# A hybrid decoder step: the first output projection, the norm and the odd input projection as one stage

## The chip, the cores and the metric

One core of a Trainium2 chip runs the whole program. The metric is device time in microseconds (us), median of several executions; lower is better. TensorE is called PE, VectorE DVE, ScalarE ACT, GpSimd POOL, and SP is the engine that issues most DMA transfers. Every engine works through its own list of instructions in order and waits on semaphores.

## The reference, cut to what matters

Two layers are computed for 1024 prompt tokens and 64 sample tokens (T = 1088 rows, D = 1024 columns, all float32). The part between the layers is:

```
mix = concat(attention * silu(ga), hgrn * silu(gb))      # layer 0, T x 1024
y   = x + mix @ w_out_even[0]                            # 1024 x 1024
h   = y * rsqrt(mean(y*y, -1) + eps) * norm_g[1]         # RMS norm
q, k, v, g = split(h @ w_in_odd[0])                      # 1024 x 6144
```

Layer 0 begins in the same way, with h from the input x and w_in_even (1024 x 4096).

## The kernel before, in words

**Stages.** The program is a row of stages with a barrier behind each: project_in "even" (L93), attention, HGRN, project_out "out0" (L1638), project_in "odd" (L93 again), and retention with the last output projection. Rows are worked in NT = 9 tiles of 128 tokens (tile 8 has 64). The contraction of 1024 is cut in 8 chunks of 128.

**Precision.** A float32 operand a is split in hi = round(a) and lo = a - hi, both in the faster format fp32r, and a product is three matmuls: hi*hi, hi*lo, lo*hi. For the 64 rows of tile 8, hi and lo stand side by side as one stationary operand of 128 columns, so two matmuls do.

**project_out_alone (out0).** SP loads the weights in 8 chunks through 4 raw buffers (L1683) and the mix tiles through 2 (L1678). ACT rounds mix tiles (L1749) and even weight chunks (L1759), DVE subtracts (L1777, L1795), POOL does both for odd chunks (L1705, L1707). PE (L1720) makes tiles 0 and 1 together, chunk by chunk, as weights come; then one tile after another, 48 matmuls of 512 columns each. Tile 8 has 32. Two pairs of PSUM banks are used in turn. DVE adds the residual x (L1784, loaded by POOL's queue, L1698), ACT's queue stores y to DRAM (L1753).

**project_in.** SP loads ident and gain, then for odd cos and sin, then x tiles into 2 buffers (L195), with halves of the first weight blocks between (L197, L200). ACT squares and sums a tile (L386) and takes the root (L389). DVE inverts it (L495) and scales the 128x1024 tile to x_n (L499). PE transposes x_n in 8 pieces of 128x128 into two PSUM tiles, turn[0] and turn[1] (L236). DVE multiplies by the gain into h_f (L425), ACT rounds it to h_hi (L326), DVE subtracts to h_lo (L430). L433 places the lo of tile 8 beside its hi. POOL splits the weights by half blocks of 128x1024 (L223 rounds, L225 subtracts); a slot is two halves, and there are 4 slots.

**Units.** The products (L242) come in units of 24 matmuls (16 for the 64 rows) that each fill one of 6 PSUM banks. The first segment of odd is "rotary": unit u covers 362 or 364 tokens as moving columns; units 0 and 1 need the first 3 tiles, 2 and 3 the first 6, 4 and 5 all nine. Units 0 to 5 use slot 0, 6 to 11 slot 1. The first segment of even is "norm" with one unit of 512 columns per tile. "Early" units are made between the transposes, as soon as their tiles are there:

```python
            for t in range(NT):
                transpose_tile(t)
                while early < min(NBANK, early_units) and tiles_of(first, early) <= t - 1:
                    if early == 0:
                        pe.wait_ge(w_split, 4 if first in BY_TOKEN else 2)
                    pe.wait_ge(lo_done, 2 * tiles_of(first, early))
                    unit(first, first_at, 0, 0, early)
                    early += 1
            pe.wait_ge(lo_done, 2 * NT + 2)
```

The rest follows in order, PE waiting for a bank to be emptied (`free`) and for w_split. Rotary units are emptied by DVE (L481 to L489).

**The order of the work** around the change is written out by hand: each engine's list is fixed, and the semaphores (m_split, full, added, turned, hi_done, lo_done, w_split) only hold it back.

Of the kernel before, what the change touches and what calls it, by code (L numbers as in the profile page):

```python
# [13 lines left out]

# [12 lines left out]
P = 128  # L27
# [62 lines left out]
NSTAGE = 3  # L90


def project_in(nc, tag, x_of, gain_dram, weight, segments, consts, qk_gain_dram=None):  # L93
# [6 lines left out]
    with nc.cleanup_on_exit(), ExitStack() as ctx:  # L100
        sb = lambda n, s, d=F32: ctx.enter_context(nc.sbuf_tensor(f"{tag}_{n}", s, d))
        sem = lambda n: nc.alloc_semaphore(f"{tag}_{n}")
        even = tag == "even"
        bank = [ctx.enter_context(nc.psum_tensor(f"{tag}_bank{i}", [P, 512], F32)) for i in range(NBANK)]
# [5 lines left out]
        x_in = sb("x_in", [P, 2, D])  # L110
        x_n = sb("x_n", [P, 2, D])
        square = sb("square", [P, D])
# [4 lines left out]
        h_f = sb("h_f", [P, 2, 4, P])  # L117
# [5 lines left out]
        stage_tm = sb("stage_tm", [P, NSTAGE, 2 * WBLK])  # L123
        if even:
            stage_fm = sb("stage_fm", [P, 2, T])
            qk_gain = sb("qk_gain", [P, 2, DA])
# [5 lines left out]
        else:  # L132
# [3 lines left out]
            rot = sb("rot", [P, 4, 364])  # L136

        const_in = sem("const_in")
        x_load = [sem("x_load0"), sem("x_load1")]
        sumsq_done, std_done, rstd_done, xn_done = sem("sumsq"), sem("std"), sem("rstd"), sem("xn")  # L140
        turned, gained, hi_done, lo_done = sem("turned"), sem("gained"), sem("hi"), sem("lo")
# [13 lines left out]
        NCONST = 16 * 4  # L155
# [15 lines left out]

        @contextmanager
        def two_by_two(engine, n):

            assert n == 1 or n % 2 == 0
            if n <= 2:
                yield [(i, i) for i in range(n)]
            else:
                with engine.Fori(0, n // 2) as i:
                    yield [(2 * i + sub, sub) for sub in range(2)]  # L180

        @block.sync
        def _(sp):
            sp.dma_start(ident[:], consts["ident"]).then_inc(const_in, 16)
            sp.dma_start(gain[:], gain_dram, allow_slow_non_contiguous=True).then_inc(const_in, 16)
            if even:
                for i in range(2):
                    sp.dma_start(qk_gain[:, i, :], qk_gain_dram[i].to_broadcast([P, DA])).then_inc(const_in, 16)
            else:
                sp.dma_start(cos[:], consts["cos"]).then_inc(const_in, 16)  # L190
                sp.dma_start(sin[:], consts["sin"]).then_inc(const_in, 16)
            for t in range(NT):
                if t >= 2:
                    sp.wait_ge(xn_done, t - 1)
                sp.dma_start(x_in[0:rows_of(t), t % 2, :], x_of(t)).then_inc(x_load[t % 2], 16)  # L195
                if t in (1, 2):
                    sp.dma_start(raw[:, t - 1, :, :], w_rows[:, 4 * (t - 1):4 * t, 0:WBLK]).then_inc(raw_in[t - 1], 16)  # L197
                if t in (3, 4):
                    sp.wait_ge(w_split, t - 2)
                    sp.dma_start(raw[:, t - 3, :, :], w_rows[:, 4 * (t - 3):4 * (t - 2), WBLK:2 * WBLK]).then_inc(raw_in[t - 3], 16)  # L200
# [8 lines left out]
        def _(pool):  # L209

            pool.sem_inc(w_used, 2)
            with pool.Fori(0, NBLK // NSLOT) as turn_of_slots:
                for slot in range(NSLOT):
# [3 lines left out]
                    for half in range(2):  # L217
                        r = raw[:, half, :, :]
                        hi = w_hi[:, slot, half * 4:half * 4 + 4, :]
                        lo = w_lo[:, slot, half * 4:half * 4 + 4, :]  # L220
                        pool.wait_ge(raw_in[half], 16 * NSLOT * turn_of_slots + 16 * slot + 16)
                        pool.sem_inc(w_at_hand, 1)
                        nc.gpsimd.tensor_copy(hi, r).then_inc(w_hi_done, 1)  # L223
                        pool.wait_ge(w_hi_done, 2 * NSLOT * turn_of_slots + 2 * slot + half + 1)
# [2325 lines left out]
```

## Time and profile before

| | us |
|---|---|
| median of 3 runs | 2255.38 (2255.22 to 2260.37) |
| the profiled execution | 2255.49 |
| its span in the profile | 2253.8 |
| PE busy | 1957.6 (87%) |
| DVE busy | 966.5 (43%) |
| POOL busy | 654.8 (29%) |
| ACT busy | 528.9 (23%) |

In the profile, an instruction has a start and a duration. A float32r matmul of 512 columns lasts 0.39 us at the full clock, but the next one starts 0.23 after it, since matmuls are pipelined; what counts is the distance of the starts. PEclk is the clock granted to PE (1.00 is 2.4 GHz, 0.50 is 1.2 GHz). "idle before <-X" is how long the engine stood still and what released it. The program has 28678 instructions.

### The profile page before, as it was taken

To read this page: it belongs to the slowest core of one execution; us is meant where nothing else is said; L and a number is where in the kernel's file an instruction comes from. 1 tells how busy PE (TensorE), PEld (TensorE's weight loads), DVE (VectorE), ACT (ScalarE), POOL (GpSimd) and SP (SyncE) were. 2 spreads that over 40 slices of the span, in tenths; PEclk is the share of its full clock that TensorE was granted. 3 is DMA by queue.
4 is the path that set the end of the run, shared out by engine and by line. 5 is a ranking of instruction groups with operands and counts; after the bars stand their busy time and mean duration, and the time that the engine had idled before them with its cause. 6 is when DMAs were issued, how large, how long until landed. Compare 5 with 4: busy or idle time off the path is not lost. (4 is left out here: it accounts for less than half of the span.)

```text
span 2253.8 us, 28678 instructions
## 1 busy us (share of the span) xinstructions
PE 1957.6 (87%) x10146; PEld 1570.9 (70%) x10146; DVE 966.5 (43%) x1465; ACT 528.9 (23%) x1018; POOL 654.8 (29%) x556
## 2 busy tenths in 40 slices
PE   5999999788787864876884999999999949999998
PEld 4788998744444534764774999888788836777776
DVE  5650001087874448893327544211100035656564
ACT  3210110166554343332103000000011122323231
POOL 2522222065553006550204322233222032212120
PEclk9999999888888986796996999999999969999999
DMA  4332221233420653112425223223322187655553
GB/s 131 109 109 79 88 87 59 81 104 121 121 93 26 192 173 98 50 52 94 161 98 175 87 87 98 90 85 108 96 82 68 49 239 217 204 182 187 185 175 117
DMA packets 209185, 262.33 MB, mean 116 GB/s; under 512 B 22901, under 2 KB 149557, under 8 KB 208821
## 3 DMA queue, kind: packets, MB, share of 16 engines
q1 hardware_dynamic: 153396, 202.15, 29.1%
q10 hardware_dynamic: 53680, 53.50, 7.3%
q0 software_dynamic: 2000, 5.25, 0.8%
q8 instruction: 67, 1.10, 0.2%
q14 instruction: 42, 0.34, 0.1%
HBM read 179.31 MB, written 79.17 MB: 115 GB/s over the span
## 5 line engine op out<-in xcount | busy, mean ns | idle before, releaser
L242 PE MATMUL odd_bank<-odd_w_hi,odd_h_hi 128*128 128x512 f32 x576 | 224.9, 390 | 2.5 <-DVE odd_stage_tm L470 2.5
L242 PE MATMUL odd_bank<-odd_w_lo,odd_h_hi 128*128 128x512 f32 x576 | 224.6, 390 | 0.0
L242 PE MATMUL odd_bank<-odd_w_hi,odd_h_lo 128*128 128x512 f32 x512 | 199.9, 390 | 0.0
L223 POOL CAST odd_w_hi<-odd_raw 128x1024 fp32r<-128x1024 f32 x48 | 53.8, 1120 | 386.7 <-PE odd_bank L242 322.7
L242 PE MATMUL even_bank<-even_h_hi,even_w_hi 128*128 128x362 f32 (+1 forms) x384 | 126.9, 330 | 4.5 <-DVE even_stage_tm L470 4.5
L242 PE MATMUL odd_bank<-odd_h_hi,odd_w_hi 128*128 128x362 f32 (+1 forms) x384 | 127.4, 332 | 2.2 <-DVE odd_h_hi L433 2.2
L242 PE MATMUL odd_bank<-odd_h_lo,odd_w_hi 128*128 128x362 f32 (+1 forms) x384 | 127.0, 331 | 0.0
L242 PE MATMUL even_bank<-even_h_hi,even_w_lo 128*128 128x362 f32 (+1 forms) x384 | 126.7, 330 | 0.0
L242 PE MATMUL even_bank<-even_h_lo,even_w_hi 128*128 128x362 f32 (+1 forms) x384 | 126.6, 330 | 0.0
L242 PEld LDWEIGHTS odd_bank<-odd_w_hi,odd_h_hi 128*128 128x128 f32 x576 | 108.5, 188 | 25.4 <-DVE odd_stage_tm L470 3.0
L242 PE MATMUL odd_bank<-odd_h_hi,odd_w_lo 128*128 128x362 f32 (+1 forms) x384 | 126.2, 329 | 0.0
L242 PE MATMUL even_bank<-even_w_hi,even_h_hi 128*128 128x512 f32 x288 | 114.7, 398 | 12.4 <-POOL even_w_lo L225 7.6
L242 PEld LDWEIGHTS odd_bank<-odd_w_lo,odd_h_hi 128*128 128x128 f32 x576 | 108.6, 188 | 22.5
L225 POOL TENSOR_TENSOR odd_w_lo<-odd_raw,odd_w_hi 128x1024 fp32r<-128x1024 f32 x48 | 117.1, 2440 | 3.8
L1539 PE MATMUL hg_sc<-hg_x 128*128 128x128 f32 x448 | 72.7, 330 | 50.7 <-DVE hg_x L1439 33.9
L242 PE MATMUL even_bank<-even_w_lo,even_h_hi 128*128 128x512 f32 x288 | 113.5, 394 | 0.0
L242 PEld LDWEIGHTS odd_bank<-odd_w_hi,odd_h_lo 128*128 128x128 f32 x512 | 96.4, 188 | 20.2
L1539 PEld LDWEIGHTS hg_sc<-hg_x 128*128 128x128 f32 x448 | 68.2, 241 | 57.9 <-issue 52.1
L647 POOL CAST ap_k_hi<-ap_sums 128x512 fp32r<-128x512 f32 (+3 forms) x96 | 48.3, 503 | 198.9 <-DVEq L788 134.6
L223 POOL CAST even_w_hi<-even_raw 128x1024 fp32r<-128x1024 f32 x32 | 36.0, 1125 | 235.1 <-PE even_bank L242 188.3
L2148 PE MATMUL rt_y<-rt_w_hi,rt_m_hi 128*128 128x512 f32 x256 | 103.3, 404 | 0.0
L242 PE MATMUL even_bank<-even_w_hi,even_h_lo 128*128 128x512 f32 x256 | 101.1, 395 | 0.0
(302 smaller groups left out, 4419.9 us busy)
## 6 DMA issues: line engine op xcount, KB each, us to landing
odd_raw<-in_w_in_odd SPq DMA_DIRECT2D x48, 512.0 KB, 3.9
even_raw<-in_w_in_even SPq DMA_DIRECT2D x32, 512.0 KB, 3.8
k_page<-in_cache_k SPq DMA_DIRECT2D x64, 256.0 KB, 3.1
v_page<-in_cache_v SPq DMA_DIRECT2D x64, 256.0 KB, 3.0
rt_s<-in_state_ret SPq DMA_DIRECT2D x32, 512.0 KB, 6.0
out_ret_sample<-rt_s SPq DMA_DIRECT2D x32, 512.0 KB, 3.2
v_tm<-odd_stage_tm ACTq DMA_DIRECT2D x64, 128.0 KB, 1.9
g_tm<-odd_stage_tm ACTq DMA_DIRECT2D x64, 128.0 KB, 1.9
```

The lines of the kernel that those rows point to most:

```text
L223: nc.gpsimd.tensor_copy(hi, r).then_inc(w_hi_done, 1)
L225: nc.gpsimd.tensor_tensor(lo, r, hi.bitcast(F32), ALU.subtract).then_inc(w_split, 1)
L242: mm = pe.matmul(out, stationary, moving, start=(j == 0), stop=(j == len(pairs) - 1))
L647: nc.gpsimd.tensor_copy(k_hi[:, m, lo:NQ], sums[:, i % NX, lo:NQ]).then_inc(carry_hi, 1)
L1539: mm = pe.matmul(sc[2 * (l % 2) + c // 4][:, c % 4, :], lhs[:, tok], rhs[:, tok], start=True, stop=True)
L2148: mm = pe.matmul(yp[half][:], a[:, r, :], b[:, r, cols], start=(r == 0 and j == 0), stop=(r == R - 1 and j == len(ops) - 1))
```

## The change

It does four things.

1. project_out_alone is gone. project_in "odd" does its work first, in the same stage: the buffers of the later part (w_hi, w_lo, stage_rot, stage_tm, rot) serve as weight and mix buffers of the output projection. y stays in x_in (and is stored to DRAM too, for the last stage).
2. The three pairs of the six banks are used for the products. Tiles 2 to 6 are made one by one; transposes of an earlier tile stand among their products. Tiles 7 and 8 are made together, chunk by chunk (row by row of the weights), so that POOL can overwrite used weight chunks with the first odd weights.
3. In both input projections the tile isn't scaled before the transpose. PE multiplies the unscaled tile by diag(rstd) (128x128), a float32 matmul, which transposes and scales at once. x_n goes.
4. h_f goes as well: ACT (with the gain as scale) and DVE read the PSUM tile in 4 pieces each per half. project_in "even" has 4 input buffers instead of 2.

The diff, cut to its core:

```diff
-        x_n = sb("x_n", [P, 2, D])
-        h_f = sb("h_f", [P, 2, 4, P])
+        nx = NX if even else 2          # NX = 4
+        diag = sb("diag", [P, 2, P])
+        def o_bank(t, n):
+            return bank[2 * (t % 3) + n]
@@ block.sync
             if even:
...
+                for t in range(NT):
+                    if t >= nx:
+                        sp.wait_ge(turned, 2 * (t - nx + 1))
+                    sp.dma_start(x_in[0:rows_of(t), t % nx, :], x_of(t)).then_inc(x_load[t % nx], 16)
+                    if t in (1, 2):
+                        load_raw(0, t - 1)
+                    if t in (3, 4):
+                        sp.wait_ge(w_split, t - 2)
+                        load_raw(1, t - 3)
             else:
+                def load_mix(t):
+                    if t >= 2:
+                        sp.wait_ge(m_split, t - 1)
+                    sp.dma_start(mix[:, t % 2, :, 0:r], ...).then_inc(mix_in[t % 2], 16)
+                for c in range(KD):
+                    if c >= NRAW:
+                        sp.wait_ge(*split_by(c - NRAW))
+                    sp.dma_start(oraw[:, c % NRAW, :], ow_rows[:, c, :]).then_inc(oraw_in[c % NRAW], 16)
+                    if c < 2:
+                        load_mix(c)
+                    if c == 2:
+                        load_consts()
+                for t in range(2, NT):
+                    load_mix(t)
+                    if t in (3, 4):
+                        load_raw(0, t - 3)
+                sp.dma_start(cos[:], ...); sp.dma_start(sin[:], ...)
+                for half in range(2):
+                    sp.wait_ge(w_split, half + 1)
+                    load_raw(1, half)
@@ block.gpsimd
+            def load_residual(t):
+                if t >= 2:
+                    pool.wait_ge(y_left[t % 2], 16 * (t // 2))
+                    pool.wait_ge(turned, 2 * (t - 2) + 2)
+                pool.dma_start(x_in[0:rows_of(t), t % 2, :], out.x_of(t)).then_inc(res_in[t % 2], 16)
+            if not even:
...
+                for t in range(2, NT):
+                    load_residual(t)
+                for slot in range(NSLOT):
+                    if slot < NSLOT - 1:
+                        pool.wait_ge(chunk_used, 2 * slot + 2)
+                    else:
+                        pool.wait_ge(o_full, NT)
+                    split_slot(0, slot)
@@ block.tensor
-                        mm = pe.transpose(turn[k][:, c, 0:r], x_n[...], ident[0:r, 0:r])
+                        mm = pe.matmul(turn[k][:, c, 0:r], x_in[0:r, t % nx, (4 * k + c) * P:(4 * k + c + 1) * P],
+                                       diag[0:r, t % 2, 0:r], start=(c == 0), stop=True, skip_group_check=True)
+            def first_chunk(t):
+                pe.wait_ge(m_split, t + 1)
+                if t >= 3:
+                    pe.wait_ge(added, t - 2)
+            def project_tiles():
+                for c in range(KD):
+                    for t in range(2):
+                        if c == 0:
+                            first_chunk(t)
+                        if t == 0:
+                            pe.wait_ge(*split_by(c))
+                        mm = chunk(t, c)
+                        if c == KD - 1:
+                            mm.then_inc(o_full, 1)
+                for t in range(2, NT - 2):
+                    first_chunk(t)
+                    for c in range(KD):
+                        mm = chunk(t, c)
+                        if c == KD - 3:
+                            transpose_tile(0 if t == 2 else t - 1)
+                    mm.then_inc(o_full, 1)
+                    if t == 2:
+                        transpose_tile(1)
+                first_chunk(NT - 2)
+                first_chunk(NT - 1)
+                for c in range(KD):
+                    mm = chunk(NT - 2, c)
+                    if c == KD - 1:
+                        mm.then_inc(o_full, 1)
+                    mm = chunk(NT - 1, c)
+                    mm.then_inc(o_full if c == KD - 1 else chunk_used, 1)
+                    if c == 4:
+                        transpose_tile(NT - 3)
+            else:
+                project_tiles()
+                early_unit(0)
+                transpose_tile(NT - 2)
+                early_unit(1)
+                transpose_tile(NT - 1)
+                for early in range(2, 4):
+                    early_unit(early)
@@ block.scalar
-                nc.scalar.copy(h_hi[:, 4 * k:4 * k + 4, ...], h_f[:, k, :, 0:r]).then_inc(hi_done, 1)
+                for c in range(4 * k, 4 * k + 4):
+                    ins = nc.scalar.activation(h_hi[:, c, ...], turn[k][:, c % 4, 0:r], ACT.Copy, scale=gain[:, c:c + 1])
+                ins.then_inc(hi_done, 1)
+            def split_hi(t):
+                act.wait_ge(mix_in[t % 2], 16 * (t // 2) + 16)
+                if t >= 2:
+                    act.wait_ge(o_full, t - 1)
+                nc.scalar.copy(m_hi[...], mix[...]).then_inc(m_hi_done, 1)
+                split_hi(0)
+                round_weights(0)
+                split_hi(1)
+                for c in range(2, KD, 2):
+                    round_weights(c)
+                act.wait_ge(const_in, NCONST)
+                split_hi(2)
+                split_hi(3)
+                for t in range(2):
+                    norm(t)
+                    store(t)
+                cast(0)
+                for t in range(4, NT):
+                    cast(t - 3)
+                    split_hi(t)
+                    norm(t - 2)
+                    store(t - 2)
+                cast(NT - 3)
+                for t in range(NT - 2, NT):
+                    norm(t)
+                    store(t)
+                cast(NT - 2)
+                cast(NT - 1)
@@ block.vector
-                dve.tensor_scalar(x_n[0:r, t % 2, :], x_in[0:r, t % 2, :], rstd[0:r, t:t + 1], None, ALU.mult)
+                dve.tensor_scalar(diag[0:r, t % 2, :], ident[0:r, :], rstd[0:r, t:t + 1], None, ALU.mult).then_inc(diag_done, 1)
+                    for c in range(4 * k, 4 * k + 4):
+                        ins = dve.scalar_tensor_tensor(h_lo[:, c, ...], turn[k][:, c % 4, 0:r], gain[:, c:c + 1],
+                                                       h_hi[:, c, ...], ALU.mult, ALU.subtract)
+                for t in range(4, NT):
+                    gain_and_split(t - 3)
+                    add(t - 2)
+                    scale(t - 2)
+                    split_lo(t)
```

## Rows read from the trace of the kernel before

**Rows 1.** The page, first part: busy time and share of each engine.

```profile
PE 1957.6 (87%) x10146; PEld 1570.9 (70%) x10146; DVE 966.5 (43%) x1465; ACT 528.9 (23%) x1018; POOL 654.8 (29%) x556
```

**Rows 2.** Stretches around the seam: us, busy of each engine, PEclk, DMA share, GB/s.

```profile
1098.50:1175.40 76.90, 74.59 (x328) 61.11 (x326) 17.75 (x24) 6.93 (x7) 3.73 (x7) 1.00 0.39 130
1175.40:1194.30 18.90, 0.00 (x0) 0.00 (x0) 4.30 (x8) 4.06 (x7) 1.60 (x2) 0.63 0.49 160
1194.30:1215.90 21.60, 9.33 (x40) 7.87 (x41) 20.42 (x23) 9.37 (x18) 14.07 (x7) 0.50 0.58 189
...
1247.00:1421.00 174.00, 174.00 (x1055) 174.00 (x1056) 77.45 (x138) 0.00 (x0) 42.42 (x24) 1.00 0.28 82
```

**Rows 3.** Timeline of PE, end of the seam: start, us, instruction, idle before and its releaser.

```profile
1246.95 0.43 PE L242 MATMUL odd_bank<-odd_h_hi,odd_w_hi 128*128 128x362 f32 x1 [2.17 <-DVE odd_h_hi L433]
```

**Rows 4.** Timeline of ACT, DVE and PE at the start of out0.

```profile
1066.23 1.04 ACT L1749 CAST out_m_hi<-out_mix 128x1024 fp32r<-128x1024 f32 x1 [9.85 <-DMA out_mix<-mix]
...
1070.60 1.04 ACT L1749 CAST out_m_hi<-out_mix 128x1024 fp32r<-128x1024 f32 x1 [3.33 <-DMA out_mix<-mix]
...
1073.34 5.35 DVE L1795 TENSOR_TENSOR out_w_lo<-out_raw,out_w_hi 128x1024 fp32r<-128x1024 f32 x2
...
1075.54 1.19 PE L1720 MATMUL out_bank<-out_w_hi,out_m_hi 128*128 128x512 f32 x2 [19.80 <-DVE out_w_lo L1795]
```

**Rows 5.** Timeline of out0: PE at tile 2; DVE's split of tile 8 and addition of tile 6.

```profile
1102.50 0.73 PE L1720 MATMUL out_bank<-out_w_hi,out_m_hi 128*128 128x512 f32 x2 [2.25 <-DVE out_xy L1784]
...
1157.95 0.69 DVE L1777 TENSOR_TENSOR out_m_hi<-out_mix,out_m_hi 128x512 fp32r<-128x512 f32 x1 [8.03 <-ACT out_m_hi L1749]
1158.56 1.28 DVE L1784 TENSOR_TENSOR out_xy<-out_bank,out_xy 128x512 f32<-128x512 f32 x2
```

**Rows 6.** Timeline of PE in the even stage: transposes between two units.

```profile
40.01 1.03 PE L236 MATMUL even_turn<-even_ident,even_x_n 128*128 128x128 f32 x8
40.80 0.47 PE L242 MATMUL even_bank<-even_w_hi,even_h_hi 128*128 128x512 f32 x1
```

**Rows 7.** Timeline of PE: 16 records of full float32 matmuls, two per matmul.

```profile
1017.50 1.95 PE L1539 MATMUL hg_sc<-hg_x 128*128 128x128 f32 x16
...
1034.50 3.64 PE L1572 MATMUL hg_o<-hg_v,hg_kd_tm 128*128 128x128 f32 x16
```

**Rows 8.** Timeline of ACT and DVE: the norm of tiles in the odd stage.

```profile
1198.83 1.05 ACT L386 ACTIVATE odd_square<-odd_x_in 128x1024 f32<-128x1024 f32 x1
...
1200.54 0.76 DVE L499 TENSOR_SCALAR odd_x_n<-odd_x_in,odd_rstd 128x1024 f32<-128x1024 f32 x1
...
1229.10 2.64 DVE L499 TENSOR_SCALAR odd_x_n<-odd_x_in,odd_rstd 128x1024 f32<-128x1024 f32 x1
```

**Rows 9.** Groups by line and shape: 128x128 operations out of PSUM, mean ns last.

```profile
L2264 ACT CAST rt_ms<-rt_tr 128x128 fp32r<-128x128 f32 x8 | 2.1, 266 | 29.4 <-PE rt_tr L2109 29.4
...
L1490 DVE SCALAR_TENSOR_TENSOR hg_state<-hg_state,hg_eb,hg_o 128x128 f32<-128x128 f32 x28 | 9.7, 348 | 1.3 <-PE hg_o L1572 0.2
```

**Rows 10.** Timeline of out0: first store of y, and the residual load behind it.

```profile
1102.64 0.34 ACTq L1753 DMA_DIRECT2D y<-out_xy  x1
...
1108.59 0.57 POOL L1698 DMA_DIRECT2D out_xy<-in_x_prompt  x1 [18.83 <-DMA y<-out_xy]
```

**Rows 11.** Timeline of PE: the even stage's pause before unit 6.

```profile
76.67 0.76 PE L242 MATMUL even_bank<-even_w_hi,even_h_hi 128*128 128x512 f32 x1 [4.15 <-DVE even_head_n L461]
...
81.08 0.43 PE L242 MATMUL even_bank<-even_w_lo,even_h_hi 128*128 128x512 f32 x1
```

**Rows 12.** Timeline of POOL in the even stage: weight halves, and PE's first product.

```profile
11.06 1.04 POOL L223 CAST even_w_hi<-even_raw 128x1024 fp32r<-128x1024 f32 x1 [10.49 <-DMA even_raw<-in_w_in_even]
12.18 2.35 POOL L225 TENSOR_TENSOR even_w_lo<-even_raw,even_w_hi 128x1024 fp32r<-128x1024 f32 x1
20.51 1.04 POOL L223 CAST even_w_hi<-even_raw 128x1024 fp32r<-128x1024 f32 x1 [5.98 <-DMA even_raw<-in_w_in_even]
...
32.42 0.79 PE L242 MATMUL even_bank<-even_w_hi,even_h_hi 128*128 128x512 f32 x1 [7.64 <-POOL even_w_lo L225]
```

More of the change, by code:

```diff
@@ L13 @@
 from contextlib import ExitStack, contextmanager
+from dataclasses import dataclass
 import numpy as np
@@ L90 @@
 NSTAGE = 3
+NX = 4
+_held = {}
+@dataclass
+class OutFirst:
+    mix_fm: object
+    weight: object
+    x_of: object
+    y_of: object
 def project_in(nc, tag, x_of, gain_dram, weight, segments, consts, qk_gain_dram=None):
@@ L216, in _ @@
                         pool.wait_ge(w_used, 2 * turn_of_slots + slot // 2 + 2)
[L217 to L224, printed above, removed]
-                        nc.gpsimd.tensor_tensor(lo, r, hi.bitcast(F32), ALU.subtract).then_inc(w_split, 1)
+                    split_slot(turn_of_slots, slot)
         @block.tensor
@@ L288, in _, with chunk @@
             early_units = UNITS[first] if first in BY_TOKEN else UNITS[first] // 2
-            for t in range(NT):
-                transpose_tile(t)
-                while early < min(NBANK, early_units) and tiles_of(first, early) <= t - 1:
-                    if early == 0:
-                        pe.wait_ge(w_split, 4 if first in BY_TOKEN else 2)
-                    pe.wait_ge(lo_done, 2 * tiles_of(first, early))
-                    unit(first, first_at, 0, 0, early)
-                    early += 1
+            def chunk(t, c):
+                hi, lo = m_hi[:, t % 2, c, :], m_lo[:, t % 2, c, :]
+                ops = ((hi, ow_hi), (hi, ow_lo), (lo, ow_hi)) if t < NT - 1 else ((hi, ow_hi), (hi, ow_lo))
+                for j, (m, w) in enumerate(ops):
+                    for n in range(2):
+                        mm = pe.matmul(o_bank(t, n)[:], m, w[:, c, n * 512:n * 512 + 512],
+                                       start=(c == 0 and j == 0), stop=(c == KD - 1 and j == len(ops) - 1))
+                return mm
@@ new lines, in early_unit @@
+            def early_unit(u):
+                if u == 0:
+                    pe.wait_ge(w_split, 4 if first in BY_TOKEN else 2)
+                pe.wait_ge(lo_done, 2 * tiles_of(first, u))
+                if not even:
+                    pe.wait_ge(added, NT - 2 + u // 2)
+                unit(first, first_at, 0, 0, u)
+            if even:
+                for t in range(NT):
+                    transpose_tile(t)
+                    while early < min(NBANK, early_units) and tiles_of(first, early) <= t - 1:
+                        early_unit(early)
+                        early += 1
+            else:
[5 more added lines that the diff above has]
+                for early in range(2, 4):
+                    early_unit(early)
+                early = 4
@@ L380, in act_unit, with norm @@
                     act.dma_start(sample[head], stage_rot[:, s, :, TP:T]).then_inc(left_fm[s], 16)
-            act.wait_ge(eps_set, 1)
-            for t in range(NT):
+            def norm(t):
                 r = rows_of(t)
-                act.wait_ge(x_load[t % 2], 16 * (t // 2 + 1))
-                nc.scalar.activation(square[0:r, :], x_in[0:r, t % 2, :], ACT.Square,
+                if even:
+                    act.wait_ge(x_load[t % nx], 16 * (t // nx + 1))
+                else:
+                    act.wait_ge(added, t + 1)
+                nc.scalar.activation(square[0:r, :], x_in[0:r, t % nx, :], ACT.Square,
                                      accum_out=ssum[0:r, t:t + 1]).then_inc(sumsq_done, 1)
@@ L408, in _ @@
                 act.wait_ge(left_fm[i], (16 if even else 48) * (fm // 2) + 16)
+            if not even:
+                act.wait_ge(y_left[0], 16 * (NT // 2 + 1))
+                act.wait_ge(y_left[1], 16 * (NT // 2))
         @block.vector
@@ L1808 @@
-_held = {}
 def retention(nc, *args):
```

346 lines of the change are left out of this document (146 added, 200 removed).

## The prediction

> **What bounds the kernel now.** I read the share of each engine first [rows 1]: TensorE (PE) is busy 87% of the span, the next engine 43%. So the kernel is a chain of stages that PE bounds, and a change pays where PE stands still or is slow. Next the stretches around the seam [rows 2]. The first output projection runs from 1075.5 to 1175.4, nearly without a pause. Then PE does nothing for 18.9 us and runs at the lower clock level (granted 0.50, which is 1.2 GHz) for 21.6 more; from 1247 on it is busy 174.0 of 174.0 us. The last part of the seam ends at 1246.95 [rows 3], 71.6 us after the products. In it lie the transposes of nine tiles in pieces, each behind VectorE (the last wait is 2.17 for L433), and, by the order of the code, four units (0 to 3) of the odd input projection. A unit of 24 matmuls takes 24 x 0.165 = 4.0 us (1055 records in 174.0 us [rows 2]), four take 15.9. The other 55.7 us are what the seam costs: the y tiles go to DRAM, a barrier, the reload, the norm. The output products stand 0.227 us apart (328 in 74.6 [rows 2]); a tile of 48 takes 10.9, a chunk of six 1.36.
>
> **Start of the merged stage.** Today PE starts at 1075.5 behind the second mix tile and then the first weight split [rows 4]: ScalarE rounds mix 0 at 1066.2 and mix 1 at 1070.6, when its transfer lands, and only then the weights. The new order is mix 0, weight chunk 0, mix 1. Chunk 0 was issued before mix 0, so I take it as landed by 1067.3: rounding to 1068.3, VectorE's subtraction until about 1071.0 (5.35 for two in its row, beside GpSimd), PE from 1071.1, 4.4 us earlier. The second tile's split, ready about 1073.4, meets PE's first six products (6 x 0.43 at the lower level). Bounds 0 (weights land late) and 5; I take 4.4.
>
> **The hand-over to tile 2.** Today a gap of 2.25 [rows 5]: PE waits for rounding, split and the addition that frees the banks. With three bank pairs the addition goes; what stays is rounding 1.04 [rows 4] plus a split of 1.2 (twice the 0.69 of half the size [rows 5], less overlap) after tile 0's last product, less the 1.36 of tile 1's last chunk: about 1.0. Gain 1.2.
>
> **The transposes become products with diag(rstd).** Eight transposes of a tile take 0.79 of PE (40.01 to 40.80 [rows 6]). The new form is a full fp32 matmul, two records for each of 128 columns. 16 such records in a row take 1.95 including the last one's drain, so about 1.75 of PE time at the upper level; at the lower one 3.64 and 3.4 [rows 7]. Seven tiles (0 to 6) now stand among the projection's products: 7 x 1.75 = 12.3 us added there. A rule speaks against this. The Trainium skill, page "TensorE: Matmul & The Clock Gate", section Terms, has transposes in transpose mode four times as fast for FP32; by it a tile's products would take 4 x 0.79 = 3.2, not 1.75. The rows of this kernel say a factor near two, and I go by them.
>
> **Is each norm done in time?** For tile t the chain after its last product is addition 1.3 [rows 5], then square to the start of the scaling 1.7 [rows 8], then diag, an operation of 128x128 and some 0.3 (0.35 for the nearest of that size [rows 9]). In all 3.3, where PE has six chunks of the next tile, 8.2 us. Gain and split of a tile are now 8 ScalarE and 8 VectorE instructions of 128x128 out of PSUM, 0.27 and 0.35 each [rows 9], overlapping to about 1.0 per half; they lie behind the next products. The residual load waits for the store two tiles back (issue 1102.64, POOL goes on 1108.59, 6 us [rows 10]) and has over 12. The first pair is the tightest. Its products end at 1099.9 - 4.4 = 1095.5, tile 2 runs from 1096.5, so transposes 0 are due at 1096.5 + 8.2 = 1104.7 and transposes 1 at 1104.7 + 1.75 + 2.7 = 1109.1. Addition 0 follows split 2 (1096.5 to 1097.8), and with the norm and a table load diag 0 is there at 1101; the halves of tile 0 are rounded from 1106.3 and split by 1108.6 and 1110, each when its bank is due. All at nothing, with 2 to 8 us of cover; without cover each us late is a us of PE.
>
> **The stall that the change adds.** Tiles 7 and 8 start together, and tile 8's mix shares its buffer with tile 6. So ScalarE may round it only when tile 6 is complete, and VectorE has addition 6 and scaling 6 (which waits for ScalarE's norm 6) queued ahead of split 8: 1.35 + 1.8 + 0.3 + 0.7 [rows 5, 8, 9] + the start of PE 0.15 = 4.3 us in which PE has nothing; transposes 6 and units wait behind it. The same length of pause in the even stage (4.15) left PE at the lower level: ten products at 0.43 instead of 0.23 [rows 11], 2.0 us. Together 6.3. Bounds: 3 (a quicker queue, no clock loss) and 9.
>
> **The end of the stage.** Products end at 1175.4 - 4.4 - 1.2 + 12.3 + 6.3 = 1188.4. Unit 0, transposes 7, unit 1, transposes 8, units 2 and 3 follow: 15.9 + 1.75 + 1.3 (64 rows) = 19.0. Diag 7 is due 4.0 after the end and ready at 2.5; its VectorE operation has only SBUF operands, and such ones take up to 2.64 instead of 0.76 beside GpSimd [rows 8], so up to 1 more, which the wait of unit 0 below covers. With the 1.0 that unit 0 waits (next part) unit 4 starts at 1208.4 instead of 1246.95. **Gain 38.5 us.** After that the stage is PE alone, as before.
>
> **The queues.** SP issues ident and gain behind weight chunk 2 (used by ScalarE at mix 2, some 15 us later), the two halves of the first odd block behind mix 3 and 4, cos and sin behind mix 8, which goes out when tile 6's mix is split, about 1152; VectorE wants them at 1203. Then SP waits for the splits from 1174 on, with only the next weight halves behind it. POOL has the residual loads ahead of the new splits; the last of them (tile 8) waits for transposes 6, some 5 us before the end of the products, and that is later than the use of chunk 1. So the new splits start only near 1182, at 3.5 us (1.04 and 2.35 [rows 12]) to 4 each, and two of them end near 1189.4: unit 0, due at 1188.4, waits 1.0 us for them (bounds 0 and 3). Unit 6 gets its four near 1197 and needs them at 1216. The old barrier, the reload and the nine x loads of SP go.
>
> **The even stage** changes too. Four input buffers let x 2 and the second weight half be asked for at once. Today that half reaches GpSimd at 20.5 after 6 us of waiting, and the fourth split ends at 32.4, which starts PE [rows 12]. With the transfers back to back (x 0, x 1 and the first half, 1.5 MB, were in by 11.06) the second half lands by 14.6, and the four splits end near 14.6 + 3.8 + 3.9 + 3.9 = 26.2. Transposes 2 end near 25, so PE starts at 26.3: 6.1 earlier. Against this stand 5 x 0.95 + 0.6 = 5.4 for transposes 3 to 8, which lie between units, and 0.5 for the smaller instructions in the pause before unit 6 [rows 11]. Sum -0.2; bounds -5 and +5.
>
> **Sum.** The profiled execution took 2255.5 (span 2253.8 and 1.7 around it), the median of the three runs is 2255.4. 2255.5 - 38.5 - 0.2 = 2216.8.
>
> **Rivals.**
> 1. The hand-overs are dearer: weights land late at the start (4.4 lost), a missed norm or two in the first pair, diag 7 and 8 behind GpSimd. Each is 1 to 5 us; for it speaks the tight first pair, against it the cover elsewhere. 7 to 19 us less gain: 2224 to 2236, middle 2229. Chance 0.17.
> 2. The products with diag take four times today's 0.79, so 3.2 a tile: 1.45 more for 9 tiles in the merged stage and 6 in the even one, some 20 us: 2237. This is the mechanism behind the rule cited above. Against it stand 16 records in 1.95. Chance 0.03.
> 3. Slower: the chain through VectorE's queue (gain and split, addition, the wait for the norm, split of the next mix tile) takes longer than PE's 12.7 us a tile (10.9 + 1.75). Then PE pauses at every tile boundary as at tile 8, 4.3 plus 2.0 of clock. For tiles 2 to 8 that is 44 us against 38.5 gained: 2261. It decides from 12.7 + 4.3 = 17 us of chain on; my sum from complete tile to split is 4.3, with the gain and split 6.5. Chance 0.03.
> 4. The seam does not close: the transposes are issued in order on PE, so a norm late for its slot in every tile would keep the 12.3 and give back half of the 55.7. 2240 or so. Chance 0.02.
> 5. More gain: the stall at tile 8 short, the clock kept, the even start 5 better: 2206. Chance 0.07, and 0.68 for the forecast's own 2209 to 2224.
>
> The range 2206 to 2236 holds case 1 and the forecast with its unknown bounds (5 at the start, 3 at the stall, 5 in the even stage). A measurement of this kernel tells about 0.3%, 7 us, from no change. Faster by more than that: all but 3, and a little of unseen trouble, 0.95; within 0.02; slower 0.03.
>
> **What would show it.** PE's first product of the merged stage near 1071; 16 records of diag products in 1.95; a pause near 1 us before tile 2; no pause over 0.5 us at tiles 3 to 7; one pause near 4.3 before tile 7 with slow products behind it; continuous PE from there, a wait of 1 us at unit 0, unit 4 near 1208; in the even stage the first product at 26 and the pause before unit 6 near 4.6. The forecast is wrong if PE waits for diag or split in each tile, or if 16 records take over 3 us.

## The result, and the profile after

The changed kernel takes **2218.74 us** (median of 4, 2217.01 to 2219.43) against 2255.3 (2254.49 to 2260.37) for the kernel before on the same chip: ratio 0.983 [0.9815, 0.9849]. Predicted were 2216.8 in a range of 2206 to 2236. A later series gave 2220.5 (2219.6 to 2233.6, 6 runs) against 2257.99, ratio 0.984 [0.9809, 0.987]. The profiled execution took 2217.01 (span 2215.2). In the profile TensorE (PE) is busy for slightly longer, and still not for the whole span:

```profile
PE 1959.9 (88%) x10290; PEld 1577.1 (71%) x10290; DVE 931.5 (42%) x1537; ACT 547.0 (25%) x1126; POOL 646.4 (29%) x556
```

PE's busy time grew by 2.3 us [rows 1]; the span fell by 38.6. So time in which PE stood still went away, and the windows of the changed kernel say where (columns as in [rows 2]):

```profile
1057.60:1069.80 12.20, 0.04 (x1) 0.04 (x1) 3.46 (x4) 3.88 (x4) 4.39 (x4) 0.50 0.98 309
1069.80:1094.00 24.20, 24.06 (x96) 19.30 (x96) 6.34 (x5) 3.40 (x5) 13.05 (x7) 0.92 0.52 173
1094.00:1161.20 67.20, 66.07 (x336) 55.75 (x336) 29.84 (x79) 28.10 (x73) 3.21 (x6) 1.00 0.45 151
1161.20:1165.30 4.10, 0.00 (x0) 0.02 (x1) 2.28 (x5) 2.05 (x4) 0.00 (x0) 1.00 0.34 140
1165.30:1186.40 21.10, 21.09 (x93) 17.48 (x94) 2.17 (x9) 2.18 (x8) 5.29 (x5) 0.92 0.08 23
1186.40:1208.00 21.60, 20.38 (x130) 19.59 (x129) 13.86 (x34) 6.89 (x22) 17.86 (x11) 1.00 0.54 166
```

From 1069.8 to 1208.0 PE is busy 131.6 of 138.2 us; between products and odd projection it had done nothing for 18.9 and been busy for only 9.33 of the next 21.6, at granted 0.50 [rows 2]. The rows of PE that answer to [rows 3 to 7, 11], from its timeline:

```profile
27.64 0.50 PE L342 MATMUL even_bank<-even_w_hi,even_h_hi 128*128 128x512 f32 x1 [1.79 <-POOL even_w_lo L292]
...
75.92 0.77 PE L342 MATMUL even_bank<-even_w_hi,even_h_hi 128*128 128x512 f32 x1 [4.42 <-DVE even_head_n L670]
...
1069.77 1.22 PE L394 MATMUL odd_bank<-odd_w_hi,odd_m_hi 128*128 128x512 f32 x2 [17.23 <-DMA odd_gain<-in_norm_g]
...
1095.04 0.74 PE L394 MATMUL odd_bank<-odd_w_hi,odd_m_hi 128*128 128x512 f32 x2 [1.17 <-DVE odd_m_lo L714]
...
1118.01 1.95 PE L336 MATMUL odd_turn<-odd_diag,odd_x_in 128*128 128x128 f32 x16
1119.71 0.71 PE L394 MATMUL odd_bank<-odd_w_hi,odd_m_hi 128*128 128x512 f32 x2
1120.27 0.62 PE L394 MATMUL odd_bank<-odd_w_lo,odd_m_hi 128*128 128x512 f32 x2
...
1130.34 0.62 PE L394 MATMUL odd_bank<-odd_w_hi,odd_m_lo 128*128 128x512 f32 x2
1130.80 1.95 PE L336 MATMUL odd_turn<-odd_diag,odd_x_in 128*128 128x128 f32 x16
...
1165.31 0.71 PE L394 MATMUL odd_bank<-odd_w_hi,odd_m_hi 128*128 128x512 f32 x2 [4.21 <-DVE odd_m_hi L714]
1165.86 0.99 PE L394 MATMUL odd_bank<-odd_w_lo,odd_m_hi 128*128 128x512 f32 x2
1166.65 1.05 PE L394 MATMUL odd_bank<-odd_w_hi,odd_m_lo 128*128 128x512 f32 x2
...
1188.49 0.43 PE L342 MATMUL odd_bank<-odd_h_hi,odd_w_hi 128*128 128x364 f32 x1 [1.22 <-POOL odd_w_lo L292]
...
1200.40 0.43 PE L342 MATMUL odd_bank<-odd_h_hi,odd_w_hi 128*128 128x362 f32 x1
...
1208.40 0.33 PE L342 MATMUL odd_bank<-odd_h_hi,odd_w_hi 128*128 128x362 f32 x1
```

Unit 2 starts at 1200.40 and, 48 products later, unit 4 at 1208.40: 38.6 earlier than [rows 3]. That equals the gain of the whole span, so nothing behind the seam gives or takes. But part of it is chance. The stage's first DMA went out at 1057.60; in the trace of before it was at 1060.82:

```profile
1057.60 0.34 SPq L259 DMA_DIRECT2D odd_stage_rot<-in_w_out_even  x1
...
1062.46 0.48 SPq L231 DMA_DIRECT2D odd_gain<-in_norm_g  x1
```

Counted from it, unit 4 came after 186.13 us before and after 150.80 now: the merged stage gives **35.3**. In the profiles of the changed kernel and the twelve runs below this first DMA lay between 1057.60 and 1078.34, though attention and HGRN, which stand ahead of it, are the same in all. That is why effects of a few us are read below from **local stretches** of one execution. I use D (the stage's first DMA), T2 (first product of tile 2) and U2 (first product of unit 2, behind transposes 8). For the changed kernel U2 - D = 142.80 and U2 - T2 = 105.36; its second profile gave 144.36 and 106.06. Up to T2, eight of the profiles have the same merged stage: T2 - D lies between 37.03 and 38.88 in them (37.44 in the changed kernel's). From T2 to U2, five have the same waits and code: 105.36 to 106.51. One execution can't tell an effect smaller than these spreads of 1.9 and 1.2 by its length alone; a wait that is there or gone can still be read from its row.

### The profile page after: what moved, and what is told of

Same layout as the page of the kernel before. It is cut to its first block and busy times, and to the rows that moved or that the text cites. A ratio compares the mean times of both kernels' runs of the same rounds, so it can differ in the third digit from the quotient of the medians.

```text
span 2215.2 us, 29001 instructions
## 1 busy us (share of the span) xinstructions
PE 1959.9 (88%) x10290; PEld 1577.1 (71%) x10290; DVE 931.5 (42%) x1537; ACT 547.0 (25%) x1126; POOL 646.4 (29%) x556
```

## The experiments

**Which part of the change pays?** Two kernels each keep one half. e1_even_only has the new even stage and the old project_out_alone and odd stage; e2_even_old is the reverse:

```diff
 # e1_even_only
-project_in(nc, "odd", ...)            # merged
+project_out_alone(nc, "out0", ...)    # as before
+project_in_old(nc, "odd", ...)
 # e2_even_old
-project_in(nc, "even", ...)
+project_in_old(nc, "even", ...)
```

> The even stage as changed, the output projection and the odd stage as before. My account of the gain puts it all at the seam: the even stage gives at most 1 us, so 2254 to 2256, no difference that can be measured, and the stretch from the first weight transfer of the output projection to unit 4 of odd stays 186.1 us. Rival: the 2.5 us by which HGRN ended earlier in the changed kernel are owed to the even stage; then 2251 to 2253.

> The merged stage as changed, the even stage as before. The seam account: 2218 to 2221, with unit 4 of odd 150.7 us after the first weight transfer of the output projection as in the changed kernel, and unit 6 of even at 76.7 instead of 75.9. Rival (the even stage has a share): 2222 to 2224.

Measured: e1 2261.65 (2255.64 to 2265.19) against 2256.23, ratio 1.001 [0.9992, 1.0027]. Its median lies above the 2254 to 2256 that I expected, but the ratio shows no change, and unit 4 of odd came 186.40 after D (186.1 expected). Unit 6 of even came at 76.23, before 76.67 [rows 11]; e2, with the old even stage, has it at 76.19. e2 2219.31 (2218.06 to 2221.66), ratio 0.9829 [0.9794, 0.9865]; U2 - D 143.54, PE's pauses behind its start within 0.1 of the changed kernel's. All of the gain that can be measured is the merged stage; the new even stage pays for itself and no more.

**The start.** The prediction had PE start when weight chunk 0 is split. The timeline of VectorE (DVE) says that this split was done at 1066.3, and PE started 3.5 later:

```profile
1065.05 1.22 DVE L718 TENSOR_TENSOR odd_w_lo<-odd_stage_rot,odd_w_hi 128x1024 fp32r<-128x1024 f32 x1
...
1161.14 1.29 DVE L726 TENSOR_TENSOR odd_x_in<-odd_bank,odd_x_in 128x512 f32<-128x512 f32 x2 [0.32 <-PE odd_bank L394]
...
1163.97 0.16 DVE L703 RECIPROCAL odd_rstd<-odd_std 128x1 f32<-128x1 f32 x1 [1.54 <-ACT odd_std L552]
1164.17 0.29 DVE L707 TENSOR_SCALAR odd_diag<-odd_ident,odd_rstd 128x128 f32<-128x128 f32 x1
1164.37 0.68 DVE L714 TENSOR_TENSOR odd_m_hi<-odd_shared,odd_m_hi 128x512 fp32r<-128x512 f32 x1
```

The row of PE at 1069.77 names gain: PE waits at its head for all constants, and SP issued gain as the seventh transfer of the stage, at 1062.46, behind three weight chunks, two mix tiles and ident, while the DMA engines were full (share 0.98 in the first window). e3_no_const_wait takes that wait out of PE's head in the odd stage; ScalarE still has it, ahead of anything that makes diag:

```diff
-            pe.wait_ge(const_in, NCONST)
+            if even:
+                pe.wait_ge(const_in, NCONST)
```

> PE's wait for ident and gain stands only in the even stage; in the merged one PE starts with the products (its transposes wait for diag anyway). If that wait alone held the first product, PE starts when chunk 0 is split, 3 us earlier (some 8.8 instead of 12.2 after the first transfer), then pauses 1 to 2 us for tile 1's split, so that unit 4 comes 1.5 to 2 us earlier; the whole 2215 to 2218. Rival: the weight chunks become the bound at once, and unit 4 doesn't move.

Measured (one execution, 2235.63, whose extra time lies ahead of the stage: D at 1078.34):

```profile
1088.07 1.19 PE L395 MATMUL odd_bank<-odd_w_hi,odd_m_hi 128*128 128x512 f32 x2 [14.79 <-DVE odd_w_lo L719]
...
1092.41 0.73 PE L395 MATMUL odd_bank<-odd_w_hi,odd_m_hi 128*128 128x512 f32 x2 [1.45 <-DVE odd_m_lo L715]
```

PE starts 9.73 after D instead of 12.17, and 0.15 after VectorE has split chunk 0 (3.5 before), so the wait was what held it. But it then runs into the second mix tile, which was due next (1.45). A wait removed uncovers the next one: of the 2.4 at the start, 1.3 are left at tile 2 (T2 - D 36.12 for 37.44; the least of the eight profiles with the wait is 37.03). At U2 0.2 is left (142.63 for 142.80), since in this execution the slow products behind the later stall went on longer (granted 0.74 over 1184.7 to 1196.0), and the edit doesn't touch those. So what it is worth alone at the end of the stage isn't shown; at tile 2 it is 0.9 to 2.8 against those eight.

**The stall before tiles 7 and 8.** The four last rows of VectorE above are the predicted chain: addition 6, the wait for norm 6, the scaling, and only then split 8; PE has nothing for 4.21. Two kernels attack it. e4_apart makes tile 8 after tile 7 instead of together with it, so PE has 48 products to do meanwhile; e5_split_first moves split 8 ahead in VectorE's queue:

```diff
 # e4_apart
-                for t in range(2, NT - 2):
+                for t in range(2, NT - 1):
...
-                first_chunk(NT - 2)
                 first_chunk(NT - 1)
                 for c in range(KD):
-                    mm = chunk(NT - 2, c)
...
-                    if c == 4:
-                        transpose_tile(NT - 3)
 # e5_split_first, in VectorE's list
                     gain_and_split(t - 3)
+                    if t == NT - 1:
+                        split_lo(t)
                     add(t - 2)
                     scale(t - 2)
-                    split_lo(t)
+                    if t < NT - 1:
+                        split_lo(t)
```

> Tiles 7 and 8 are made one after the other, as tiles 2 to 6. My account of the stall: mix 8 is split beside tile 7, so the 4.2 us pause and the slow products behind it (1.9) go, 6.1 us; GpSimd still gets chunk 1 free some 5.5 us before the end of the products, so unit 0 waits 1 to 2 us as now. Unit 4 comes 5 to 6 us earlier, the whole 2211 to 2214. Rival, the reason for making them together: the weights are freed too late, unit 0 waits over 5 us, and nothing is won: 2217 to 2220.

> VectorE splits mix 8 ahead of addition 6 and scaling 6 instead of behind them; nothing else changes. If its queue makes the 4.2 us pause, the pause is what rounding and split alone take, 0.62 + 0.68 and some 0.2: about 1.5 us, and the products behind it stay at 0.23 (pauses of 1.2 left the clock up). From the first product of tile 2 to unit 4 some 4.5 us less. Rival: the pause comes from ScalarE or from the mix transfer and stays 4.2.

e4: 2217.28 (2214.47 to 2217.59), ratio 0.9813 [0.9778, 0.9849]. Its windows and PE's row at unit 0:

```profile
1099.18:1185.30 86.12, 86.12 (x432) 72.59 (x432) 34.99 (x94) 32.76 (x86) 8.85 (x11) 1.00 0.41 136
```
```profile
1187.09 0.43 PE L342 MATMUL odd_bank<-odd_h_hi,odd_w_hi 128*128 128x364 f32 x1 [1.76 <-POOL odd_w_lo L292]
```

PE is busy 86.12 of 86.12 us at granted 1.00; U2 - T2 is 99.82, 5.5 less, and unit 0 waits 0.5 more for weights, since the chunks come free later. So the stall with its slow products costs 6.1, as the prediction had it (6.3). The total is not the 2211 to 2214 that I expected, but the stage also began late in this profile (D at 1062.15, 4.55 later). e5 (one execution, 2221.39, D at 1063.85):

```profile
1170.17 0.70 PE L394 MATMUL odd_bank<-odd_w_hi,odd_m_hi 128*128 128x512 f32 x2 [1.69 <-DVE odd_m_hi L714]
```
```profile
1170.17:1180.00 9.83, 9.83 (x43) 8.09 (x44) 1.40 (x4) 1.45 (x3) 0.00 (x0) 1.00 0.13 53
```

This is a pause of 1.69 (1.5 expected) with granted 1.00 behind it, where 4.21 was followed by products some 0.42 apart until 1169.2; U2 - T2 = 101.22, 4.1 less (4.5 expected), of which 2.5 is the shorter pause and 1.6 the clock. Both kernels fit the account of the prediction: the price is the pause and, nearly half as much again, the slow products that follow it.

**Unit 0's weights.** GpSimd's timeline in the changed kernel:

```profile
24.11 1.04 POOL L290 CAST even_w_hi<-even_raw 128x1024 fp32r<-128x1024 f32 x1 [2.10 <-DMA even_raw<-in_w_in_even]
...
1180.94 0.53 POOL L298 DMA_DIRECT2D odd_x_in<-in_x_sample  x1 [21.52 <-PE odd_turn L336]
1181.46 1.05 POOL L290 CAST odd_w_hi<-odd_raw 128x1024 fp32r<-128x1024 f32 x1
...
1186.06 2.37 POOL L292 TENSOR_TENSOR odd_w_lo<-odd_raw,odd_w_hi 128x1024 fp32r<-128x1024 f32 x1
```

GpSimd stood 21.52 behind the residual load of tile 8, which waits for transposes 6, though chunks 0 and 1 were free before. e8_residual_sp lets SP issue that one load:

```diff
 # SP, behind cos and sin
+                sp.wait_ge(y_left[0], 16 * ((NT - 1) // 2))
+                sp.wait_ge(turned, 2 * (NT - 3) + 2)
+                sp.dma_start(x_in[0:TS, 0, :], out.x_of(NT - 1)).then_inc(res_last, 16)
 # GpSimd
-                for t in range(2, NT):
+                for t in range(2, NT - 1):
                     load_residual(t)
```

> The residual of tile 8 is asked for by SP instead of GpSimd's queue, so that GpSimd can split the first odd weights as soon as chunk 1 of the last pair is used. If the wait for transposes 6 in GpSimd's queue sets the 1.2 us wait of unit 0, the splits start near 13 us after the pause's end less 7 (at 6 instead of 16 us), unit 0 doesn't wait, unit 4 comes 1.2 earlier. Rival: the weights aren't there or the new pause moves to transposes 7 (diag 7), same unit 4.

GpSimd's first split now starts 7.3 us after the end of the stall instead of 16.2, and the wait of 1.2 at unit 0 is gone, in one execution (2220.98); U2 - T2 is 104.82, only 0.5 less, as the slow products behind the stall lasted 0.7 longer this time.

**The even stage.** The fourth weight half was asked for only at 19.01, because SP first waited to load x 4 into a freed buffer. e7_even_order puts both halves ahead of x 4:

```diff
-                    if t in (3, 4):
-                        sp.wait_ge(w_split, t - 2)
-                        load_raw(1, t - 3)
+                    if t == 3:
+                        for half in range(2):
+                            sp.wait_ge(w_split, half + 1)
+                            load_raw(1, half)
```

> Even stage: SP asks for the second half of weight block 1 before x tile 4, whose wait for transposes 0 held it in the queue until 18.6. The half is asked for at 18.1, the fourth split ends 0.9 us earlier, PE's first product of even comes at 26.7 to 27.2 instead of 27.6, bound then by transposes 2. Unit 6 0.5 to 0.9 earlier. Rival: PE's start is bound by transposes 2 already, no change.

Unit 6 starts at 74.05 instead of 75.92 (total 2222.27 in one execution):

```profile
22.23 1.04 POOL L291 CAST even_w_hi<-even_raw 128x1024 fp32r<-128x1024 f32 x1 [0.24 <-DMA even_raw<-in_w_in_even]
...
25.77 0.50 PE L343 MATMUL even_bank<-even_w_hi,even_h_hi 128*128 128x512 f32 x1
...
74.05 0.77 PE L343 MATMUL even_bank<-even_w_hi,even_h_hi 128*128 128x512 f32 x1 [4.43 <-DVE even_head_n L671]
```

That is 1.9 less, where I expected 0.5 to 0.9. The fourth split begins at 22.23 instead of 24.11, and PE's first product comes at 25.77 instead of 27.64. SP asked for the half only about 1 us earlier; the other 0.9 was won between the issue and the split, and why isn't shown (x 4 no longer goes ahead of it).

**Diag products against transposes.** e9_transpose keeps the merged stage but scales rows to x_n and transposes them in transpose mode, with x_n in a buffer that is free then:

```diff
-                        mm = pe.matmul(turn[k][:, c, 0:r], x_in[...], diag[0:r, t % 2, 0:r], start=(c == 0), stop=True, ...)
+                        mm = pe.transpose(turn[k][:, c, 0:r], x_n[0:r, t % 2, ...], ident[0:r, 0:r])
...
-                dve.tensor_scalar(diag[0:r, t % 2, :], ident[0:r, :], rstd[0:r, t:t + 1], None, ALU.mult)
+                dve.tensor_scalar(x_n[0:r, t % 2, :], x_in[0:r, t % 2, :], rstd[0:r, t:t + 1], None, ALU.mult)
```

> The merged stage scales the tile on VectorE and transposes it on PE in transpose mode, as the kernel before did, instead of the product with diag; the even stage keeps diag. A tile's transposes take 0.8 of PE instead of 1.9: 7 x 1.1 among the products, 1.1 and 1.4 for tiles 7 and 8, against it 0.5 more in the pause before tile 7. Unit 4 comes 9 to 10 us earlier, the whole 2208 to 2211. Rival: VectorE's dearer scaling (0.76, up to 2.6 beside GpSimd) makes PE wait for the tiles 0, 1, 7 and 8, and half of it is lost: 2212 to 2216.

Measured: 2220.87 (2216.49 to 2227.24), ratio 0.984 [0.9817, 0.9864], where 2208 to 2211 was expected: no faster than the changed kernel in total. PE's rows:

```profile
1128.15 1.04 PE L341 MATMUL odd_turn<-odd_ident,odd_stage_rot 128*128 128x128 f32 x8
...
1140.03 1.03 PE L341 MATMUL odd_turn<-odd_ident,odd_stage_rot 128*128 128x128 f32 x8
...
1172.26 1.19 PE L399 MATMUL odd_bank<-odd_w_hi,odd_m_hi 128*128 128x512 f32 x2 [4.73 <-DVE odd_m_hi L722]
...
1205.58 0.43 PE L341 MATMUL odd_turn<-odd_ident,odd_stage_rot 64*128 64x64 f32 x4 [0.59 <-DVE odd_h_lo L641]
```

A tile step is 11.88 (1128.15 to 1140.03) instead of 12.79, 0.91 less. In both kernels the 48 products of a step stand 0.229 apart and take 10.99 (in the changed kernel 44 of them in the 10.07 from 1120.27 to 1130.34), so the transposes take 0.89 and the diag form 1.80. But the scaling of 1024 columns lies in the chain of the stall (4.73 instead of 4.21), the products behind it were slow for longer (1.3 in this execution), and 0.59 + 0.60 of waits appear at tile 8. U2 - T2 = 100.04, 5.3 less where 9 to 10 was expected.

**Put together.** c3_lead takes e3, e5, e7 and e8, and lets the first tile of each pair run ahead of the second (by one chunk at tiles 0 and 1, by two at 7 and 8), so that PE has products while the second mix tile is split. c4_lead_transpose adds e9. a1_after is the changed kernel again, beside them on the same chip:

```diff
+            def ahead(t0, t1, lead):
+                order = [(t0, c) for c in range(lead)]
                 for c in range(KD):
-                    for t in range(2):
+                    order += [(t0, c + lead)] * (c + lead < KD) + [(t1, c)]
+                return order
...
+                for t, c in ahead(0, 1, 1):
...
+                for t, c in ahead(NT - 2, NT - 1, 2):
```

> The changed kernel once more, as the measure for the two beside it: 2217 to 2220, unit 2 of odd begins 142.8 us after the first weight transfer of the output projection.

> All that the single runs showed, together: no constants wait for PE, mix 8 split first, residual 8 by SP, the even weight half before x 4, and in both pairs of tiles the first runs ahead (one chunk in the first pair, two in the last), so that the second's split lies beside products. If each pause is what the single runs made of it: first product 9.7 instead of 12.2 after the first transfer, no pause at tiles 1, 2, 7, 8 and unit 0; 2.4 + 1.2 + 6.1 + 1.2 less, unit 2 at 131.9 instead of 142.8; 1.9 in the even stage; in all 12.8 less than the changed kernel: 2206. Rival: the early start runs into the weight chunks, which come as before, and 2 to 4 us of it come back: 2208 to 2210.

> The same with transposes of the scaled tile in the merged stage instead of products with diag. Each takes 0.97 of PE instead of 1.91 (tile steps of 11.85 and 12.79), nine of them 8.5 less if none waits: unit 2 at 124, the whole 2198. Rival: transposes 8 wait for VectorE (1.2 as in the single run) and those of tiles 0 and 1 too; 4 us come back, 2202.

| | us | ratio to before | U2 - D |
|---|---|---|---|
| a1_after | 2220.5 | 0.984 [0.9809, 0.987] | 144.36 |
| c3_lead | 2210.47 | 0.979 [0.9758, 0.9822] | 132.12 |
| c4_lead_transpose | 2206.37 | 0.9767 [0.9738, 0.9795] | 126.85 |
| c5_mixed | 2201.52 | 0.9744 [0.9722, 0.9766] | 124.92 |

The stretch of c3 came out as expected (132.12 for 131.9), its total didn't (2210.47 for 2206; the rival had 2208 to 2210). c4 missed both (126.85 for 124, 2206.37 for 2198): its rival, waits at transposes 8, is part of it. c5, tried after these two, stands in the last row.

The windows of c3 show the waits at the second mix tile and before tiles 7 and 8 filled:

```profile
1068.10:1094.00 25.90, 25.54 (x98) 20.06 (x99) 10.46 (x7) 5.40 (x6) 16.45 (x9) 0.89 0.64 203
1094.00:1180.00 86.00, 86.00 (x435) 72.83 (x434) 34.22 (x93) 33.54 (x87) 11.57 (x12) 1.00 0.43 142
1180.00:1207.40 27.40, 27.40 (x177) 27.10 (x176) 16.05 (x38) 5.44 (x19) 19.30 (x11) 1.00 0.45 144
```

In c4, PE waited before transposes 8, and VectorE's timeline says for what:

```profile
1183.26 0.43 PE L346 MATMUL odd_turn<-odd_ident,odd_stage_rot 64*128 64x64 f32 x4 [2.88 <-DVE odd_h_lo L652]
...
1184.30 0.43 PE L346 MATMUL odd_turn<-odd_ident,odd_stage_rot 64*128 64x64 f32 x4 [0.60 <-DVE odd_h_lo L652]
```
```profile
1179.08 2.88 DVE L726 TENSOR_SCALAR odd_stage_rot<-odd_x_in,odd_rstd 64x1024 f32<-64x1024 f32 x1
1181.99 2.16 DVE L652 SCALAR_TENSOR_TENSOR odd_h_lo<-odd_turn,odd_gain,odd_h_hi 128x128 fp32r<-128x128 f32 x8
```
```profile
1184.60:1188.00 3.40, 3.40 (x15) 3.34 (x13) 3.24 (x13) 0.98 (x5) 3.32 (x3) 0.58 0.24 70
```

The scaling of tile 8 took 2.88 beside GpSimd's splits, with gain and split 7 queued behind it, and the products after the pause ran at granted 0.58. This is what the diag form buys: its operation of 128 columns. So c5_mixed uses transposes for tiles 0 to 6, where VectorE has time, and diag for 7 and 8:

```diff
-                        if even:
+                        if even or t >= NT - 2:
                             mm = pe.matmul(turn[k][:, c, 0:r], ... diag ...)
```

> Leading tiles with transposes of scaled rows for tiles 0 to 6, but products with diag(rstd) for tiles 7 and 8. In the kernel with transposes everywhere, VectorE scaled the 1024 columns of tile 8 in 2.88 us beside GpSimd, the gain and split of tile 7 stood behind it in VectorE's queue, and PE waited 2.88 + 0.60 for it before and inside transposes 8. Theory (this VectorE work is the cover that the diag form buys, 0.34 instead of 2.88): both waits vanish; transposes 7 and 8 cost 0.9 more each, so from the stage's first DMA to the first product behind transposes 8 it takes 126.85 - 3.5 + 1.9 = 125.3 us, and total is 1 to 3 us lower with the slow products behind the wait gone too. Rival (the wait comes from GpSimd holding VectorE's gain and split themselves, 2.16 either way): a wait of 2 us or more stays before transposes 8, and the stage takes 128 or more.

```profile
1181.02 0.39 DVE L724 TENSOR_SCALAR odd_diag<-odd_ident,odd_rstd 64x128 f32<-64x128 f32 x1
1182.21 2.16 DVE L652 SCALAR_TENSOR_TENSOR odd_h_lo<-odd_turn,odd_gain,odd_h_hi 128x128 fp32r<-128x128 f32 x8 [0.81 <-ACT odd_h_hi L502]
```
```profile
1095.00:1185.80 90.80, 90.80 (x455) 76.99 (x453) 44.49 (x107) 37.76 (x102) 22.05 (x18) 1.00 0.47 156
1185.80:1209.00 23.20, 23.20 (x141) 23.18 (x141) 12.34 (x28) 1.05 (x5) 8.86 (x5) 1.00 0.40 122
```

The waits are gone: PE is busy all of the 114 us from 1095.0 to 1209.0 at granted 1.00, U2 - D = 124.92 (expected 125.3). With 2201.52 (2196.16 to 2204.78) it has the lowest ratio of all kernels run, 0.9744. Against the changed kernel's 0.984 it is some 1% better; its interval, and c4's, lie below the changed kernel's, c3's overlaps it. Neighbours in the table differ by less than their intervals can tell; there only the local stretches speak, from one execution each.

## Why the prediction was right

The time came out 1.9 above the forecast, well inside its own range, by the mechanism named: the idle seam is filled with products, and the price is longer transposes and one stall. Term by term, from the stage's first DMA:

- **Start of PE: missed in part.** The step "Chunk 0 was issued before mix 0 ... PE from 1071.1, 4.4 us earlier" looked only at weights and mix. Those were even earlier than forecast: chunk 0 was split 8.7 after the stage's first DMA, where the prediction had 10.2. PE's own wait for the constants, gain being behind six other transfers, ended last: PE started 2.55 earlier instead of 4.4. The order in which SP issues gain was in the text ("behind weight chunk 2"), but only ScalarE's use of it was costed. e3 shows that the wait was real and that a further one, of 1.45, lay under it.
- **Products of tiles 0 and 1**: 24.1 us instead of 24.7 (1075.54 to the gap before 1102.50 [rows 4, 5]), 0.6 not foreseen.
- **Gap before tile 2**: 1.0 predicted, 1.17 measured (2.25 before).
- **Diag products**: 1.75 predicted, 1.80 measured, so the reading of [rows 7] was right. What was off is the products around them: they stand 0.229 apart, not the 0.227 of the output projection before, and a tile of 48 takes 10.99 instead of 10.88; why isn't shown. Together that is 1.91 added to a tile instead of 1.75, 1.1 us more for tiles 0 to 6. For tile 8 the diag products took 1.93 instead of 1.3: 64 rows cost no less than 128. The Trainium skill, page "TensorE: Matmul & The Clock Gate", section Terms, has FP32 transposes in transpose mode four times as fast; that rule would give 3.2 for the diag form, an estimate. e9 and the changed kernel measure 0.89 against 1.80, a factor of two, so the rule doesn't hold here and rival 2 falls.
- **Norms in time**: right. No pause over 0.5 at tiles 3 to 6, none ahead of any transposes.
- **Stall**: 4.3 predicted, 4.21 measured. Slow products behind: 2.0 predicted. The 80 products and transposes 6 from 1165.31 to the end at 1187.27 took 21.96; at 0.2289 and 1.80 they would take 20.1, so 1.9.
- **Unit 0**: 1.0 predicted, 1.22 measured, for the reason given.
- **Even stage**: -0.2 predicted. In the profile unit 6 came 0.75 earlier, e1 shows no change in the total. PE's first product at 27.64 (26.3 predicted) was held by the fourth half.

Sum of what went against the forecast: 1.85 + 0.2 + 1.1 + 0.8 (tiles 7 and 8) + 0.2 = 4.1; for it 0.6 and 0.2 at the stall. The rest, 3.3, is what the stage fell short (150.8 instead of 147.6 after its first DMA), and the 3.2 by which the stage began earlier in this execution covered it up. That is luck for the most part: only 0.9 of it was there when the even stage ended, and the rest arose in attention and HGRN, which the change doesn't touch. The local account is the honest one: 35.3 gained where 38.5 was claimed.

Of the rivals, rival 1 happened in small (the start); rival 3, a pause at each tile boundary, needed a chain of 17 us and has no pause to show; rival 4 likewise; rival 5's parts (no stall, clock kept, better even start) are real, but took another kernel: c3 to c5.

## What to carry to other kernels

A barrier between two stages that PE bounds costs more than the barrier: reload, norm and the slow clock behind the pause. Filling it with the first stage's own products was worth 35 us here, though it made PE's work longer. In a merged order look at the pairs that start together and at the last tile: let one product run ahead while the other's operand is made, and put the operation that PE waits for first in its engine's queue. When you cost a start, list **every** semaphore at the head of the engine's list, constants too.

Choose the form of a step by the engine that has time in that place: transposes with a VectorE scaling where VectorE is idle, the diag product where VectorE's queue holds PE.

## What the runs showed of the hardware that I had not expected

- After a pause of 4.21 the time at granted 0.50 was not the same in each execution of the same code: from the end of the stall to transposes 6 it took 13.13 us in the changed kernel's first profile, 13.81 in its second, 13.68 in e2 and 14.27 in e3. Pauses of 1.69 (e5) were followed by granted 1.00, the 2.88 + 0.60 of c4 by 0.58.
- Eight full fp32 products of 64 rows with a 64-column diag take no less than eight of 128: 1.93 from their start to the next product in the changed kernel (tile 8), 1.71 for tile 7 (1192.59 to 1194.30). The operand that PE loads has 128 columns in both, and PE's 16 weight loads take 1.86 and 1.92; whether these set the pace isn't shown.
- The same products of 512 columns stood 0.2267 us apart in the output projection before and 0.2289 in the merged stage, both at granted 1.00. No run separates the cause.
- VectorE's scaling of 1024 columns took 2.88 beside GpSimd for the 64 rows of tile 8. Even the diag operation of 128 columns, 0.29 in the chain of the stall, took 1.94 in c3 where it met a GpSimd split:

```profile
1180.00 1.94 DVE L718 TENSOR_SCALAR odd_diag<-odd_ident,odd_rstd 128x128 f32<-128x128 f32 x1
```

It cost nothing there, as transposes 7 were due at 1183.51.

- The stages between 432 and the merged one, whose code is the same in all kernels, took up to 19 us more in one execution than in another (from 432.5 to 1057.60 in the changed kernel's profile, from 434.5 to 1078.34 in e3's). A change worth 2 us can't be seen in the total there.
